# Down projection of a decoder layer: two more Strassen k pairs in its first pair of column groups, and its activation sums made by GpSimd

## The chip, the cores and the metric

The kernel runs on one core of one Trainium2 chip. The metric is the device time of one execution in microseconds. TensorE (PE in the profile) multiplies; its weight loads are a row of their own (PEld) and overlap its matmuls. VectorE (DVE), ScalarE (ACT) and GpSimd (POOL) work element by element, SyncE (SP) issues DMAs. Each engine runs its own instructions in the order of the program, and they wait for each other by semaphores.

## What is computed

One hybrid decoder layer over 256 tokens of width 2048: a mixer (attention heads beside a gated short convolution), cross-attention into 256 memory tokens, and a dense SwiGLU feed-forward layer, each with an RMS norm ahead of it and a residual add, and a last RMS norm. The change is in the last product:

```python
D_MODEL = 2048
D_FF = -(-(8 * D_MODEL) // (3 * 256)) * 256      # 5632
def swiglu(h, w_gate, w_up, w_down):
    return (jax.nn.silu(h @ w_gate) * (h @ w_up)) @ w_down
...
        x = x + swiglu(h, w_gate[l], w_up[l], w_down[l])
    return rms_norm(x, g_final)
```

## The kernel before

**Products.** A float32 product is made of three matmuls on rounded operands: high part times high part, high times low, low times high. A weight tile `raw` (128 partitions, two k blocks of 512 columns, 512 KB) comes by DMA from one stream; ACT rounds it to `whi` (line 1141), DVE subtracts `wlo = raw - whi` (line 1602), and PE multiplies. `raw`, `whi` and `wlo` are rings of four buffers (`RING`). ACT's cast of step v waits until PE has used step v-4; DVE's split waits for the cast; SP loads the next tile into a slot of `raw` when its last reader on DVE is done. ACT and DVE run `LEAD` = 2 steps ahead in their programs.

**The down projection.** Its k axis has 44 blocks of 128, in 22 pairs (numbered 0 to 21); the 2048 output columns are four groups of 512, taken as two pairs of groups, one after the other. `DOWN_ORDER` is an order written out by hand, one tuple for each pair of groups: "D8" is k pair 8 in the plain way, two steps (one for each group) of 12 matmuls; "A18" and "B18" are one such step each. "S0" is k pair 0 by Strassen's scheme: the 2 x 2 blocks (two k blocks and two token tiles on one side, two k blocks and two column groups on the other) are multiplied with seven products in place of eight, of three matmuls each: 21 matmuls in place of 24.

**An S step** has four parts, each a step of the rings, with 1, 2, 2 and 2 products. For part 0 ACT casts half a tile, and DVE makes a weight sum in `raw` (line 1597), the split (1602) and a second sum (1605). Part 1 has a split of a whole tile and then a third sum, `wsum` (1609). Part 2 casts and splits what now stands in the second tile, part 3 casts and splits `wsum`. SP loads into the slot of the first tile when `wsum` is made, and into that of the second when part 2 is split. Part 0 of the next S step needs both of these next tiles.

**Activation forms.** The S steps also need sums of the activations `fhi + flo`. They are made in four batches of two k pairs (`FORM_BATCH`): `down_sums(b)` makes a 128 x 1024 sum into `silu` (line 1634) and four 128 x 256 sums into `dsum` (1637, 1638, 1640, 1642), `down_forms(b)` on ACT casts them (1170, 1171), and `down_lows(b)` on DVE makes their low parts (1649, 1650). `FORMS_AT = {step: batch}` sets the place: after step i on DVE the sums, after step i+1 on ACT the casts, after step i+2 on DVE the low parts. PE waits for a batch (`d_lo`) at part 0 of the S steps. Batch b's sums wait for the low parts of batch b-1. POOL has no work in this stage until two small roots at the very end (line 479).

After the last S step of a pair of groups, `down_combine` adds the products up on DVE; the plain steps that follow in the order run beside it.

Of the kernel before, what the change touches and what calls it, by code (L numbers as in the profile page):

```python
# [21 lines left out]
TT = SEQ // P  # L22
# [11 lines left out]
KS = 2  # L34
# [17 lines left out]
G_DN = G_FF + 2 * NFC  # L52
# [19 lines left out]

DOWN_QUADS = 8
FORM_BATCH = 2
DOWN_ORDER = (("D6", "D7", "D8", "S0", "D9", "S1", "D10", "D11", "S2", "D12", "S3", "D13", "D14", "S4", "D15", "S5",
               "D16", "D17", "D18", "D19", "D20", "D21"),
              ("D8", "D9", "D10", "S0", "D11", "S1", "D12", "S2", "D13", "S3", "D14", "S4", "D15", "S5", "D16", "S6",
               "D17", "S7", "A18", "A19", "A20", "A21", "B18", "B19", "B20", "B21"))
DOWN = []
DOWN_TILES = []  # L80
for pair, order in enumerate(DOWN_ORDER):
    for name in order:
        q = int(name[1:])
        if name[0] == "S":
            n = len([1 for place in DOWN if place[4] == 0])
# [10 lines left out]
             for g in range(4)]  # L96
DOWN_BANKS = (2, 4, 0, 6)
PRODUCT_BANKS = ((0, 1, 7, 6), (2, 3, 4, 5))
FORMS_AT = {0: 0, 14: 1, 28: 2, 50: 3}
SQUARES_AT = {PAIR_AT[1] + 1: 0, PAIR_AT[1] + 2: 1, GROUP_END[2] + 2: 2}  # L100
ADDS_AT = {at - 1: g for at, g in SQUARES_AT.items()}
GAINS_AT = {PAIR_AT[1] + 2: 0, PAIR_AT[1] + 3: 1, GROUP_END[2] + 3: 2}
# [46 lines left out]
def build(nc, stream, x, xT, mem, memT, params, pos, inv_freq, g_final, out):  # L149
    f32, f32r, i32 = mybir.dt.float32, mybir.dt.float32r, mybir.dt.int32  # L150
    ALU, ACT, AX = mybir.AluOpType, mybir.ActivationFunctionType, mybir.AxisListType
    ds = bass.ds
    ctx = ExitStack()
    with ctx:
# [3 lines left out]
        def sb(name, shape, dt=f32, at=None):  # L158

            size = 4 * int(np.prod(shape[1:]))  # L160
            spot = place if at is None else at
            line = LINE if size >= LINE else 64
            where = -(-spot[0] // line) * line
            spot[0] = where + -(-size // 64) * 64
            return nc.alloc_sbuf_tensor_at(name, shape, dt, offset=where)
# [6 lines left out]
        def sem(name):  # L172
            return ctx.enter_context(nc.semaphore(name))
# [88 lines left out]
        fhi = sb("fhi", [P, FF // P, SEQ], f32r, at=fat)  # L262
        flo = sb("flo", [P, FF // P, SEQ], f32r, at=fat)
        silu = sb("silu", [P, TT, GC], at=fat)
# [9 lines left out]
        dsum = sb("dsum", [P, QUAD_PARTS, FORM_BATCH, P], at=sums_at)  # L274
        junk2 = sb("junk2", [P, GC], at=sums_at)
        assert sums_at[0] <= fat[0]
        dsrc = silu[:].rearrange("p t n -> p (t n)").rearrange("p (n k t m) -> p n k t m", n=FORM_BATCH, k=KS, t=TT)
# [50 lines left out]
        d_src, d_sums, d_made, d_hi, d_lo = (sem(n) for n in ("d_src", "d_sums", "d_made", "d_hi", "d_lo"))  # L328
# [17 lines left out]
        def await_out(eng, g, gi=0):  # L346

            eng.wait_ge(evacuated[g % 2], gi + (g // 2 + 1))
# [69 lines left out]
        def _(pool):  # L418
# [12 lines left out]
            def root(n):  # L431

                pool.wait_ge(var_ready, n + 1)
                nc.gpsimd.tensor_tensor(rstd[:, n, :], vpe[:, n, :], mhalf[:], ALU.pow).then_inc(rstd_ready, 1)
# [39 lines left out]
                                            ALU.subtract).then_inc(merged_conv, 1)  # L474
            root(2)
            root(3)
            for t in range(TT):
                pool.wait_ge(fvar_ready, t + 1)
                nc.gpsimd.tensor_tensor(frstd[:, t:t + 1], fvar[:, t:t + 1], mhalf[:, 0:1], ALU.pow).then_inc(frstd_ready, 1)
# [402 lines left out]
        def _(act):  # L882
# [12 lines left out]
            def unit(u, k, col, hi, ui=0, uk=0):  # L895

                act.wait_ge(unit_T, ui + (u + 1))
                bank = ps[:, unit_bank(u), :].rearrange("p (k t) -> p k t", k=KS)
                if col is None:
                    done = nc.scalar.activation(hi[:, ds(uk + k, KS), :], bank, ACT.Copy)  # L900
                else:
                    if U_H3 <= u < U_H3 + QUADS:
                        for n in range(KS):
                            nc.scalar.activation(araw[:, u - U_H3, n], bank[:, n, :].rearrange("p (t m) -> p t m", t=TT),
                                                 ACT.Copy, scale=gain(col + k + n))
                    for n in range(KS):
                        done = nc.scalar.activation(hi[:, k + n, :], bank[:, n, :], ACT.Copy, scale=gain(col + k + n))
                done.then_inc(unit_hi, 1)
# [318 lines left out]
            for i in range(len(DOWN)):  # L1227
                down_cast(i + LEAD)
                if i == LEAD:
                    act.wait_ge(step_used, V_DN)  # L1230
                    act.dma_start(gfin[:], g_final.partition_broadcast(P)).then_inc(gfin_loaded, 16)
                    for n in range(2 * (NFC - 1), 2 * NFC):
                        unit(U_FF + n, KS * n, None, fhi)
                if i - 1 in FORMS_AT:
                    down_forms(FORMS_AT[i - 1])
                for pair in range(2):
# [28 lines left out]
        def _(dve):  # L1265
            vec = nc.vector
# [278 lines left out]
            for j in range(J_XO + 1, J_FF):  # L1545
                split(j + LEAD)
                n = j - J_XO
# [74 lines left out]
                    r, pair, q, n, part = DOWN[i]  # L1622
                    part_split(V_DN + i, J_DN + r, part, DOWN_SUMS + 3 * n)

            def down_sums(b):

                k = slice(2 * KS * b, 2 * KS * (b + 1))
                flat = silu[:].rearrange("p t n -> p (t n)")
                a11, a21, a12, a22 = (dsrc[:, :, k_, t, :] for k_ in range(KS) for t in range(TT))
                if b:  # L1630
                    dve.wait_ge(d_lo, b)
                else:
                    await_out(dve, G_DN - 1)
                vec.tensor_tensor(flat, fhi[:, k, :].rearrange("p k t -> p (k t)").bitcast(f32),
                                  flo[:, k, :].rearrange("p k t -> p (k t)").bitcast(f32), ALU.add).then_inc(d_src, 1)
                dve.wait_ge(d_src, b + 1)
                vec.tensor_tensor(dsum[:, 0], a21, a22, ALU.add).then_inc(d_sums, 1)
                vec.tensor_tensor(dsum[:, 2], a21, a11, ALU.subtract)
                dve.wait_ge(d_sums, 2 * b + 1)
                vec.tensor_tensor(dsum[:, 1], dsum[:, 0], a11, ALU.subtract).then_inc(d_sums, 1)  # L1640
                dve.wait_ge(d_sums, 2 * b + 2)
                vec.tensor_tensor(dsum[:, 3], a12, dsum[:, 1], ALU.subtract).then_inc(d_made, 1)

            def down_lows(b):

                here = slice(FORM_BATCH * b, FORM_BATCH * (b + 1))
# [91 lines left out]

            for i in range(len(DOWN)):
                down_split(i + LEAD)  # L1740
                if i in FORMS_AT:
                    down_sums(FORMS_AT[i])
                if i == LEAD:
                    for n in range(2 * (NFC - 1), 2 * NFC):
                        unit(U_FF + n, KS * n, None, fhi, flo)
                if i - 2 in FORMS_AT:
                    down_lows(FORMS_AT[i - 2])
                for pair in range(2):
                    if i == LAST_QUAD[pair] + QUAD_PARTS:
                        down_combine(pair)  # L1750
                if i in ADDS_AT:
                    for t in range(TT):
                        add_result(ADDS_AT[i], t)
                if i in GAINS_AT:
                    dve.wait_ge(gfin_loaded, 16)
                    for t in range(TT):
                        dve.wait_ge(part_ready, TT * GAINS_AT[i] + t + 1)
                        gain_result(GAINS_AT[i], t)
# [66 lines left out]
```

## Time and profile before

| | us |
|---|---|
| median of 3 runs | 1200.52 (1200.32 to 1200.54) |
| the profiled execution, its own time | 1199.66 |
| its span, first to last instruction | 1198.0 |
| busy: PE, DVE, ACT, POOL | 1186.2, 930.4, 673.6, 83.5 |
| mean granted TensorE clock | 0.998 of full speed |

A matmul's row in the timeline shows when it began and how long it was in the pipeline (0.39 us); the next one begins 0.23 us later, so matmuls overlap and the distance between starts is what one costs. For the same reason a short pause of PE does not show as idle time, but as a longer distance between two starts. The same goes for DVE: a row of 1.22 us is followed by the next 1.14 us after its start.

### The profile page before, as it was taken

What the parts mean: (1) busy time and instruction counts of PE and PEld (TensorE: products, weight loads), DVE (VectorE), ACT (ScalarE), POOL (GpSimd) and SP (SyncE); (2) the same over time, 40 slices, a digit from 0 to 9 for tenths busy, and PEclk for the clock granted to TensorE, in tenths of its full rate; (3) what the DMA queues carried; (4) which work ended last, traced back from release to release, by engine and by line L of the source; (5) the groups of instructions that cost most, each with busy time, mean ns of one, the idle gap of its engine ahead of it and who ended that gap; (6) DMA issues with size and microseconds to landing.
All of it is one profiled execution on the core that took longest, in us unless ns stands there. A gap on an engine that the chain in (4) does not pass through costs nothing.

```text
span 1198.0 us, 16405 instructions
## 1 busy us (share of the span) xinstructions
PE 1186.2 (99%) x5421; PEld 983.2 (82%) x5421; DVE 930.4 (78%) x1171; ACT 673.6 (56%) x881; POOL 83.5 (7%) x89
## 2 busy tenths in 40 slices
PE   9999999999999999999999999999999999999997
PEld 8888888888888888788888888888888888888885
DVE  5755555557855666999899899989989989978886
ACT  5665555446644575666556555655555555545553
POOL 0042332200210000000000000000000000000000
PEclk9999999999999999999999999999999999999999
DMA  9865455556555544465666567556656666665663
GB/s 339 295 211 173 162 175 177 173 175 225 163 191 182 189 158 141 148 222 176 203 201 199 186 199 229 169 196 205 210 181 204 209 212 199 214 218 173 202 206 141
DMA packets 65851, 234.52 MB, mean 196 GB/s; under 512 B 7696, under 2 KB 8464, under 8 KB 65424
## 3 DMA queue, kind: packets, MB, share of 16 engines
q1 hardware_dynamic: 63072, 225.60, 57.4%
q10 hardware_dynamic: 2736, 8.35, 1.9%
q8 instruction: 26, 0.43, 0.2%
q14 instruction: 17, 0.14, 0.0%
HBM read 231.83 MB, written 2.10 MB: 195 GB/s over the span
## 4 chain that ended last, share of the span: by engine, by line
PE 92%; DVE 4%; DMA 1%; ACT 1%; issue 1%; SPq 0%; POOLq 0%; POOL 0%; ACTq 0%; DVEq 0%
PE ps L489 24%; PE ps L491 24%; PE ps L490 23%; PE ps L732 6%; PE ps L734 6%; PE ps L733 6%; DVE wlo L1602 2%; DMA raw<-w_stream 1%; PE ps L521 1%; DVE wsum L1609 0%; ACT whi L1141 0%; PE ps L604 0%; PE ps L559 0%; PE ps L564 0%; PE ps L688 0%
## 5 line engine op out<-in xcount | busy, mean ns | idle before, releaser
L1141 ACT ACTIVATE whi<-raw 128x1024 fp32r<-128x1024 f32 (+1 forms) x309 | 303.7, 992 | 214.6 <-PE ps L491 94.2
L1602 DVE TENSOR_TENSOR wlo<-raw,whi 128x1024 fp32r<-128x1024 f32 (+1 forms) x309 | 345.3, 1137 | 25.2 <-ACT whi L1141 24.4
L1271 DVE TENSOR_TENSOR wlo<-raw,whi 128x1024 fp32r<-128x1024 f32 x160 | 198.7, 1245 | 112.7 <-ACT whi L893 112.5
L489 PE MATMUL ps<-whi,ahi 128*128 128x512 f32 x600 | 235.6, 393 | 0.0
L491 PE MATMUL ps<-whi,alo 128*128 128x512 f32 x600 | 233.7, 390 | 0.0
L490 PE MATMUL ps<-wlo,ahi 128*128 128x512 f32 x600 | 233.5, 389 | 0.0
L893 ACT ACTIVATE whi<-raw 128x1024 fp32r<-128x1024 f32 x160 | 168.4, 1058 | 107.1 <-PE ps L491 94.7
L489 PE MATMUL ps<-whi,bhi 128*128 128x512 f32 x448 | 180.1, 402 | 0.8 <-DVE wlo L1271 0.7
L491 PE MATMUL ps<-whi,blo 128*128 128x512 f32 x448 | 175.1, 391 | 0.0
L490 PE MATMUL ps<-wlo,bhi 128*128 128x512 f32 x448 | 174.5, 389 | 0.0
L491 PEld LDWEIGHTS ps<-whi,alo 128*128 128x128 f32 x600 | 112.6, 188 | 23.7
L490 PEld LDWEIGHTS ps<-wlo,ahi 128*128 128x128 f32 x600 | 112.7, 188 | 22.8
L489 PEld LDWEIGHTS ps<-whi,ahi 128*128 128x128 f32 x600 | 112.7, 188 | 22.6
L491 PEld LDWEIGHTS ps<-whi,blo 128*128 128x128 f32 x448 | 84.1, 188 | 18.3
L489 PEld LDWEIGHTS ps<-whi,bhi 128*128 128x128 f32 x448 | 84.2, 188 | 17.6 <-issue 1.6
L490 PEld LDWEIGHTS ps<-wlo,bhi 128*128 128x128 f32 x448 | 84.3, 188 | 16.4
L489 PE MATMUL ps<-whi,fhi 128*128 128x512 f32 x240 | 93.7, 390 | 0.2 <-DVE wlo L1602 0.2
L491 PE MATMUL ps<-whi,flo 128*128 128x512 f32 x240 | 93.4, 389 | 0.0
L490 PE MATMUL ps<-wlo,fhi 128*128 128x512 f32 x240 | 93.4, 389 | 0.0
L1141 ACT ACTIVATE whi<-wsum 128x1024 fp32r<-128x1024 f32 x47 | 49.9, 1062 | 68.5 <-PE ps L491 49.0
L1602 DVE TENSOR_TENSOR wlo<-wsum,whi 128x1024 fp32r<-128x1024 f32 x47 | 57.6, 1225 | 36.3 <-ACT whi L1141 35.6
L1609 DVE TENSOR_TENSOR wsum<-raw 128x1024 f32<-128x1024 f32 x47 | 57.2, 1217 | 0.0
(244 smaller groups left out, 1489.9 us busy)
## 6 DMA issues: line engine op xcount, KB each, us to landing
raw<-w_stream SPq DMA_DIRECT2D x422, 512.0 KB, 4.1
res<-x_in ACTq DMA_DIRECT2D x4, 512.0 KB, 8.0
stage<-mem_in ACTq DMA_DIRECT2D x4, 512.0 KB, 6.4
proj<-mem_T ACTq DMA_DIRECT2D x2, 1024.0 KB, 9.4
stage<-x_T SPq DMA_DIRECT2D x7, 256.0 KB, 6.9
y_out<-res SPq DMA_DIRECT2D x4, 320.0 KB, 3.0
raw<-w_stream SPq DMA_DIRECT2D x4, 256.0 KB, 4.7
gfin<-g_final ACTq DMA_DIRECT2D x1, 1024.0 KB, 4.8
```

The source lines that it names most:

```text
L489: nc.tensor.matmul(bank, lhsT=a_h, rhs=w_h, start=start, stop=False)
L490: nc.tensor.matmul(bank, lhsT=a_h, rhs=w_l, start=False, stop=False)
L491: return nc.tensor.matmul(bank, lhsT=a_l, rhs=w_h, start=False, stop=stop)
L521: done = nc.tensor.transpose(bank[:, n, t * P:(t + 1) * P], src[:, t, (k + n) * P:(k + n + 1) * P], ident[:])
L732: nc.tensor.matmul(ps[:, bank, :], lhsT=a[0], rhs=w[0], start=start, stop=False)
L733: nc.tensor.matmul(ps[:, bank, :], lhsT=a[0], rhs=w[1], start=False, stop=False)
L734: return nc.tensor.matmul(ps[:, bank, :], lhsT=a[1], rhs=w[0], start=False, stop=stop)
L893: nc.scalar.activation(tile_pair(whi, j), tile_pair(raw, j), ACT.Copy).then_inc(hi_ready, 1)
L1141: nc.scalar.activation(whi_here, src, ACT.Copy).then_inc(hi_ready, 1)
L1271: vec.tensor_tensor(tile_pair(wlo, j), tile_pair(raw, j), tile_pair(whi, j).bitcast(f32), ALU.subtract).then_inc(lo_ready, 1)
L1602: vec.tensor_tensor(lo_here, src, hi_here.bitcast(f32), ALU.subtract).then_inc(lo_ready, 1)
L1609: vec.tensor_tensor(wsum[:].rearrange("p (h n) -> p h n", h=2), both, b22.unsqueeze(1).to_broadcast([P, 2, GC]), ALU.subtract).then_inc(w_ ...
```

## The change

The first tuple of `DOWN_ORDER` holds eight S steps in place of six: k pairs 6 and 7 move from D to S. Its start is D8 to D11 in place of D6 to D8, and from S0 on each S step is followed by one D step, up to S7. The batches of forms move with it, to steps 3, 11, 23 and 35. The sums of all four batches are made by GpSimd, with the same waits. The casts on ACT and the low parts on DVE stay where `FORMS_AT` puts them.

```diff
-DOWN_ORDER = (("D6", "D7", "D8", "S0", "D9", "S1", "D10", "D11", "S2", "D12", "S3", "D13", "D14", "S4", "D15", "S5",
-               "D16", "D17", "D18", "D19", "D20", "D21"),
+DOWN_ORDER = (("D8", "D9", "D10", "D11", "S0", "D12", "S1", "D13", "S2", "D14", "S3", "D15", "S4", "D16", "S5",
+               "D17", "S6", "D18", "S7", "D19", "D20", "D21"),
...
-FORMS_AT = {0: 0, 14: 1, 28: 2, 50: 3}
+FORMS_AT = {3: 0, 11: 1, 23: 2, 35: 3}
...
+            def down_sums(b):
+
+                k = slice(2 * KS * b, 2 * KS * (b + 1))
+                flat = silu[:].rearrange("p t n -> p (t n)")
+                a11, a21, a12, a22 = (dsrc[:, :, k_, t, :] for k_ in range(KS) for t in range(TT))
+                if b:
+                    pool.wait_ge(d_lo, b)
+                else:
+                    await_out(pool, G_DN - 1)
+                nc.gpsimd.tensor_tensor(flat, fhi[:, k, :].rearrange("p k t -> p (k t)").bitcast(f32),
+                                  flo[:, k, :].rearrange("p k t -> p (k t)").bitcast(f32), ALU.add).then_inc(d_src, 1)
+                pool.wait_ge(d_src, b + 1)
+                nc.gpsimd.tensor_tensor(dsum[:, 0], a21, a22, ALU.add).then_inc(d_sums, 1)
...
+            for b in range(len(FORMS_AT)):
+                down_sums(b)
...
-                if i in FORMS_AT:
-                    down_sums(FORMS_AT[i])
```

On POOL, the difference at the end of its program (names before the arrow are written, those behind it read); the five rows of a batch come four times, ahead of the last roots:

```order
 L434 TENSOR_TENSOR rstd<-vpe,mhalf 128x2 x2
-L479 TENSOR_TENSOR tail<-tail,mhalf 128x1 x2
+L486 TENSOR_TENSOR silu<-fhi,flo 128x1024
+L489 TENSOR_TENSOR dsum<-silu 128x256
+L490 TENSOR_TENSOR dsum<-silu 128x256
+L492 TENSOR_TENSOR dsum<-dsum,silu 128x256
+L494 TENSOR_TENSOR dsum<-silu,dsum 128x256
```

So POOL now has twenty instructions beside the first pair of groups.

On DVE, before, from the split of S1's last part (`wlo<-wsum,whi`) on: the sums of batch 1 after one split of D10, and its low parts two splits later, between D10 and D11:

```order
L1602 TENSOR_TENSOR wlo<-wsum,whi 128x1024
L1602 TENSOR_TENSOR wlo<-raw,whi 128x1024
L1634 TENSOR_TENSOR silu<-fhi,flo 128x1024
L1637 TENSOR_TENSOR dsum<-silu 128x256
L1638 TENSOR_TENSOR dsum<-silu 128x256
L1640 TENSOR_TENSOR dsum<-dsum,silu 128x256
L1642 TENSOR_TENSOR dsum<-silu,dsum 128x256
L1602 TENSOR_TENSOR wlo<-raw,whi 128x1024 x2
L1649 TENSOR_TENSOR flo<-dsum,fhi 128x2x128
L1650 TENSOR_TENSOR dfl<-dsum,dfh 128x3x256
```

On DVE, now, from the split of S1's part 1 on (line 1623 is the split, 1630 `wsum`, 1651 and 1652 the low parts):

```order
L1623 TENSOR_TENSOR wlo<-raw,whi 128x1024
L1630 TENSOR_TENSOR wsum<-raw 128x1024
L1651 TENSOR_TENSOR flo<-dsum,fhi 128x2x128
L1652 TENSOR_TENSOR dfl<-dsum,dfh 128x3x256
L1623 TENSOR_TENSOR wlo<-raw,whi 128x1024
L1623 TENSOR_TENSOR wlo<-wsum,whi 128x1024
L1623 TENSOR_TENSOR wlo<-raw,whi 128x1024 x2
```

The sums are gone, and the low parts of batch 1 now stand inside an S step, between its parts 1 and 2; those of batches 2 and 3 stand likewise inside S3 and S5, those of batch 0 ahead of S0.

On ACT, before, around the forms of batch 1, which stand in a row of plain casts of D10 and D11:

```order
L1141 ACTIVATE whi<-raw 128x1024 x2
L1170 ACTIVATE fhi<-dsum 128x2x128
L1171 ACTIVATE dfh<-dsum 128x3x256
L1141 ACTIVATE whi<-raw 128x1024 x2
L1141 ACTIVATE whi<-raw 128x512
```

On ACT, now:

```order
L1162 ACTIVATE whi<-raw 128x512
L1191 ACTIVATE fhi<-dsum 128x2x128
L1192 ACTIVATE dfh<-dsum 128x3x256
L1162 ACTIVATE whi<-raw 128x1024 x2
L1162 ACTIVATE whi<-wsum 128x1024
```

They now stand inside S1, between the casts of its parts 0 and 1 (inside S3 and S5 for batches 2 and 3).

## Rows read from the trace of the kernel before

**Rows 1.** Page, busy time by engine: us, share of the span, instructions.

```profile
PE 1186.2 (99%) x5421; PEld 983.2 (82%) x5421; DVE 930.4 (78%) x1171; ACT 673.6 (56%) x881; POOL 83.5 (7%) x89
```

**Rows 2.** Timeline of PE, down projection: start, duration, line, tiles, idle before.

```profile
993.04 0.39 PE L491 MATMUL ps<-whi,flo 128*128 128x512 f32 x1
993.42 0.50 PE L489 MATMUL ps<-whi,fhi 128*128 128x512 f32 x1
...
1019.16 0.39 PE L491 MATMUL ps<-whi,flo 128*128 128x512 f32 x1
1019.73 0.50 PE L489 MATMUL ps<-whi,fhi 128*128 128x512 f32 x1 [0.18 <-DVE wlo L1602]
1020.07 0.40 PE L490 MATMUL ps<-wlo,fhi 128*128 128x512 f32 x1
```

**Rows 3.** Timeline of DVE, first pair of groups: low parts, sums, splits.

```profile
968.52 0.41 DVE L1649 TENSOR_TENSOR flo<-dsum,fhi 128x256 fp32r<-128x256 f32 x1
...
969.72 1.22 DVE L1602 TENSOR_TENSOR wlo<-raw,whi 128x1024 fp32r<-128x1024 f32 x1
...
989.42 1.22 DVE L1634 TENSOR_TENSOR silu<-fhi,flo 128x1024 f32<-128x1024 f32 x1
...
992.14 1.22 DVE L1602 TENSOR_TENSOR wlo<-raw,whi 128x1024 fp32r<-128x1024 f32 x1
```

**Rows 4.** Timeline of ACT around the forms of batch 1.

```profile
992.26 0.42 ACT L1170 ACTIVATE fhi<-dsum 128x256 fp32r<-128x256 f32 x1 [3.11 <-DVE dsum L1642]
...
993.32 1.99 ACT L1141 ACTIVATE whi<-raw 128x1024 fp32r<-128x1024 f32 x2
```

**Rows 5.** Timeline of DVE, second pair of groups: S0, D11, S1, D12, S2.

```profile
1087.82 1.23 DVE L1602 TENSOR_TENSOR wlo<-raw,whi 128x1024 fp32r<-128x1024 f32 x1 [1.15 <-ACT whi L1141]
...
1090.60 1.22 DVE L1602 TENSOR_TENSOR wlo<-raw,whi 128x1024 fp32r<-128x1024 f32 x1 [0.42 <-ACT whi L1141]
...
1100.81 1.22 DVE L1602 TENSOR_TENSOR wlo<-raw,whi 128x1024 fp32r<-128x1024 f32 x1
...
1106.93 0.69 DVE L1597 TENSOR_TENSOR raw<-raw 128x512 f32<-128x512 f32 x1
...
1111.01 1.22 DVE L1602 TENSOR_TENSOR wlo<-raw,whi 128x1024 fp32r<-128x1024 f32 x1
```

**Rows 6.** Timeline of ACT, same stretch: casts for part 0 of S steps.

```profile
1095.89 0.63 ACT L1141 ACTIVATE whi<-raw 128x512 fp32r<-128x512 f32 x1 [0.56 <-DMA raw<-w_stream]
...
1106.20 0.63 ACT L1141 ACTIVATE whi<-raw 128x512 fp32r<-128x512 f32 x1 [0.68 <-DMA raw<-w_stream]
...
1147.80 1.58 ACT L1141 ACTIVATE whi<-raw 128x512 fp32r<-128x512 f32 x2 [1.47 <-DMA raw<-w_stream]
```

**Rows 7.** Timeline of PE's weight loads: the first of part 2 of S0, of S1.

```profile
1093.78 0.19 PEld L732 LDWEIGHTS ps<-whi,fhi 128*128 128x128 f32 x1
...
1103.98 0.19 PEld L732 LDWEIGHTS ps<-whi,fhi 128*128 128x128 f32 x1
```

**Rows 8.** Timeline of POOL in the attention stage, beside rows 9.

```profile
74.73 0.74 POOL L441 TENSOR_TENSOR rtmp<-proj,sin 128x256 f32<-128x256 f32 x1
75.42 1.73 POOL L441 TENSOR_TENSOR rtmp<-proj,cos 128x256 f32<-128x256 f32 x1
...
99.09 1.66 POOL L441 TENSOR_TENSOR rtmp<-proj,cos 128x256 f32<-128x256 f32 x1
```

**Rows 9.** Timeline of DVE in the same stretch.

```profile
74.88 1.67 DVE L1271 TENSOR_TENSOR wlo<-raw,whi 128x1024 fp32r<-128x1024 f32 x1 [2.01 <-ACT whi L893]
...
97.98 0.16 DVE L1411 TENSOR_TENSOR small<-small 128x2 f32<-128x2 f32 x1 [1.97 <-ACT osc L1011]
98.93 1.23 DVE L1271 TENSOR_TENSOR wlo<-raw,whi 128x1024 fp32r<-128x1024 f32 x1 [0.58 <-ACT whi L893]
100.07 0.70 DVE L1416 TENSOR_TENSOR small<-small 128x2 f32<-128x2 f32 x1
```

**Rows 10.** Page, DMA issues: KB each, median us from issue to landing.

```profile
raw<-w_stream SPq DMA_DIRECT2D x422, 512.0 KB, 4.1
```

More of the change, by code:

```diff
@@ L476, in _ @@
             root(3)
+            def down_sums(b):
[10 more added lines that the diff above has]
+                nc.gpsimd.tensor_tensor(dsum[:, 0], a21, a22, ALU.add).then_inc(d_sums, 1)
+                nc.gpsimd.tensor_tensor(dsum[:, 2], a21, a11, ALU.subtract)
+                pool.wait_ge(d_sums, 2 * b + 1)
+                nc.gpsimd.tensor_tensor(dsum[:, 1], dsum[:, 0], a11, ALU.subtract).then_inc(d_sums, 1)
+                pool.wait_ge(d_sums, 2 * b + 2)
+                nc.gpsimd.tensor_tensor(dsum[:, 3], a12, dsum[:, 1], ALU.subtract).then_inc(d_made, 1)
+            for b in range(len(FORMS_AT)):
+                down_sums(b)
             for t in range(TT):
@@ L1623, in down_split @@
                     part_split(V_DN + i, J_DN + r, part, DOWN_SUMS + 3 * n)
[L1625 to L1642, printed above, removed]
             def down_lows(b):
```

## The prediction, made before the changed kernel was run

> **What bounds the kernel.** I read the busy times first: PE is busy for 1186.2 of 1198.0 us [rows 1], so only what shortens PE's work, or makes it wait, counts. Then the timeline of PE: starts of matmuls are 0.227 us apart (from rows 7: part 2 of S1 begins 10.20 us after part 2 of S0, and 21 + 24 = 45 matmuls lie between; 10.20 / 45). Two places in the first pair of groups are wider: 0.38 us between starts and then 0.33, and 0.57 and then 0.34 [rows 2]. That is 0.25 and 0.45 us of waiting, in sum 0.7, each time for a split of DVE. So PE has almost no slack to win, and the question is how far ahead of it DVE runs in the S steps. That I read from the second pair of groups, where eight S steps alternate with D steps without any forms between them: the new order of the first pair, undisturbed.
>
> **The change, part by part.**
>
> 1. *Matmuls.* Two k pairs take 21 in place of 24: 2 x 3 x 0.227 = **-1.4 us** on PE. Its cover, DVE and ACT, is the subject of the rest.
>
> 2. *Sums leave DVE.* A batch holds DVE from 989.42 to 992.14, 2.7 us [rows 3]. The two waits of [rows 2] fall right behind batches 1 and 2; with the sums gone they go: **-0.7 us**. Before the first S step nothing else is late: eight plain steps give the splits time.
>
> 3. *The chain that paces S steps in a row.* PE does an S and a D step in 10.20 us. But part 0 of an S step waits for a tile whose DMA is issued when part 2 of the S step before is split. That split ends at 1100.81 + 1.22 = 1102.03 [rows 5], ACT's next part-0 cast begins, out of an idle time ended by the DMA, at 1106.20 [rows 6], 4.2 us later (a load takes 4.1 [rows 10]), DVE's next part 0 at 1106.93, and its part 2 ends at 1111.01 + 1.22 = 1112.23 [rows 5]. From 1106.20 to 1147.80 are four periods [rows 6], 10.4 us each. So the chain DMA, ACT, DVE, DMA takes 0.1 to 0.2 us more than PE, has no idle time to give, and what delays it is not made up before the S steps end. Before, the first pair had a second D step after every other S; now none. Seven periods at 0.15: 1.0 us.
>
> 4. *Low parts move into the chain.* They take 968.52 to 969.72, 1.2 us [rows 3]. Batches 1, 2, 3 now stand between parts 1 and 2 of S1, S3, S5, ahead of the split that releases the DMA: 3 x 1.2 = 3.6 us. Batch 0 lies ahead of S0, where there is room: 0.
>
> 5. *Casts of the forms move into the chain.* They take 992.26 to 993.32, 1.06 us [rows 4], between ACT's casts of parts 0 and 1. DVE's part 0 covers most: it keeps DVE until 2.5 us after ACT's part-0 cast began (1106.20 to about 1108.74, three half tiles), and cast, forms and cast need 0.5 + 1.06 + 1.15 = 2.7. 0.2 each, 0.6 us.
>
> 6. *GpSimd against DVE.* Rows 8 and 9 go together. POOL's instruction of 74.73 ran; DVE's split of 74.88 took 1.67 in place of 1.22 us, so it got going at 75.33, 0.60 after POOL's start. POOL's next took 1.73 in place of 0.74, so it waited until 76.41, 1.08 after the split got going. The second place is the same: POOL's of 99.09 waits 0.92, to 100.01, and DVE's small sum of 100.07, right behind its split, takes 0.70 in place of 0.16. So an instruction of one holds back the other until it is through (0.60 us for 128 x 256 on POOL, 1.08 for a split on DVE), and they take turns even when DVE has the next one ready. All of DVE's instructions in S steps are of the kind held back there. For POOL's 128 x 1024 sum no row exists: between 0.6 (if the hold doesn't grow) and 4 x 0.60 = 2.4; I take 2.3, since POOL's time must grow with the elements. A batch then holds DVE back for up to 2.3 + 4 x 0.6 = 4.7 us, against 2.7 that it took on DVE itself. What DVE can absorb is its idle time.
>
> The Trainium skill ("SBUF — State Buffer", "Who interferes with whom") speaks against this change: a DVE instruction with two SBUF inputs and a GpSimd instruction that reads SBUF exclude each other for a whole instruction. By it the long sum holds DVE for all of its time, as I take it; if the hold were 0.6 us it would be the second rival below. The rows agree on the exclusion, for short ones.
>
>    - Batch 0 starts when the last `up` is done, beside plain steps. Each DVE step has over 1 us of idle time there: 0.
>    - Batch 1 is released by the low parts of batch 0, just ahead of S0, so it runs through S0's parts 0 to 2. DVE's idle time in them is 1.15 + 0.42 = 1.6 us [rows 5]: 4.7 - 1.6 = 3.1 us later at part 2.
>    - Batches 2 and 3 are released inside S1 and S3, just ahead of part 2. DVE does that split, then the long sum holds it, then they take turns through part 3, two plain splits and the next part 0. DVE's own work to there is 3 x 1.14 = 3.4 us, POOL's 2.3 + 3 x 0.6 = 4.1: 7.5, where the chain has 4.9 (1102.03 to 1106.93). That is 2.6, and 0.3 net for the fifth sum inside part 0 (it can start as soon as the cast is there): 2.9 each, 5.8 us. POOL's own waits hurt nobody: each batch is done some 10 us before ACT casts it.
>
>    Sum of delays on the chain, from part 2 of S0 to part 2 of S7: 1.0 + 3.6 + 0.6 + 3.1 + 5.8 = 14.1 us. PE's slack there: S0's part 2 is split at 1090.60 + 1.22 = 1091.82 [rows 5], PE's first weight load of it is at 1093.78 [rows 7]: 1.95 us. What is more, PE waits: 14.1 - 1.95 = **+12.1 us**.
>
> After S7 six plain steps follow and `down_combine`, as before; 6 x 2.7 us of PE cover its 5 us.
>
> Sum: -1.4 - 0.7 + 12.1 = **+10.0 us**. On the profiled execution's own 1199.66 this is 1209.7; it lies 0.86 under the median of the runs, so 1210.5 for the median.
>
> **The rivals.**
>
> *No hold on DVE, chain still tight* (12%): terms 3 to 5 stay, 5.2 - 1.95 = 3.3 us of waiting, sum +1.2: 1201.7. Against it stand both pairs of rows in [rows 8, 9].
>
> *A short hold* (18%): every POOL instruction holds DVE for 0.6 us, the long one too. Batch 1: 3.0 - 1.6 = 1.4. Batches 2, 3: 3.4 + 2.4 - 4.9 + 0.3 = 1.2 each. 5.2 + 1.4 + 2.4 = 9.0, less 1.95 = 7.1; sum +5.0: 1205.5. For it: no row shows a longer hold.
>
> *The chain has room* (5%): a load into a freed tile lands soon enough for DVE to catch up in each period, and DVE isn't held. It decides where the chain's period falls under 10.2 us by what the forms add, 1.4 us for each two S steps, that is where loads land 0.7 us sooner than in [rows 6, 10]. Then only terms 1 and 2 are left: -2.1, 1198.4. That is 0.18%, and no route in this profile gains more, so even the kindest case is hardly faster.
>
> *A longer hold* (8%): POOL slower than in proportion, or its steps late as well, and delays that also move the DMAs of plain tiles: over 1213.5.
>
> The forecast itself, 1207.5 to 1213.5, has 57%: the hold of the long sum between 1.8 and 2.7 us moves three batches by 2 us, and the period's excess of 0.1 to 0.2 by 0.7.
>
> **The numbers.** 1210.5 us. The range, 1202.0 to 1214.0, takes in the short hold and most of the rest. About 0.2% (2.4 us) is what a measurement of this kernel can tell from no change. Faster by more: 3%. Within it: 14% (no hold, the chain has room). Slower: 83%.
>
> **What would show it.** PE's waits for the split should go from 2 to a dozen or so, most at `wlo` of parts 2 and 3 of S1 to S5, by some 12 us; none in the second pair of groups. POOL's long sum should take over 2 us, its short ones 0.7 or up to 1.9 where they wait, and DVE's splits beside them up to 3.5 in place of 1.22. If PE's waits lie at parts 2 only and DVE's rows keep their 1.22, the no-hold rival is right. If batches 2 and 3 leave no wait at part 3, the hold is short. I am wrong altogether if part-0 casts in the first pair are not preceded by a wait for the DMA or for DVE.

## The result: slower by 7.8 us, with the profile after

| | before | changed |
|---|---|---|
| median, us (4 runs each) | 1200.42 (1199.21 to 1200.54) | 1208.24 (1207.64 to 1209.28) |
| the profiled execution's own time, us | 1199.66 | 1208.20 |
| its span, us | 1198.0 | 1206.0 |
| mean granted TensorE clock | 0.998 | 0.998 |

The ratio is 1.0070, with a 95% interval of 1.0058 to 1.0082. The forecast was 1210.5 us in a range of 1202.0 to 1214.0.

The page of the changed kernel, busy time by engine as in [rows 1]:

```profile
PE 1186.4 (98%) x5415; PEld 980.5 (81%) x5415; DVE 944.1 (78%) x1161; ACT 676.4 (56%) x885; POOL 119.5 (10%) x109
```

DVE has ten instructions fewer than before and is busy for 13.7 us longer. PE has six matmuls fewer and the same busy time, since a short pause of it does not show as idle, in a span that is 8 us longer. What PE waited for is seen in the waits of its weight loads in the down projection (what was waited for, us in total, times, longest), here of the changed kernel:

```profile
PEld ps L753 <- DVE wlo L1623: 10.5, 8, 2.1
PEld ps L510 <- DVE wlo L1623: 0.9, 2, 0.4
```

Before, the same view of the same stretch has one line:

```profile
PEld ps L489 <- DVE wlo L1602: 1.0, 2, 0.6
```

From the distances between the ends of PE's steps, the waits of the changed kernel take 10.3 us: 0.64 at part 2 of S0; 1.07 and 1.97 at parts 2 and 3 of S1; 0.45 at part 2 of S2; 1.50 and 1.98 in S3; 0.50 in S4; 1.44 in S5; twice 0.3 at the D step behind S1 and S3; 0.1 in small ones. There is none in S6 and S7 and none in the second pair of groups. So -1.4 (matmuls), -0.7 (the two waits of [rows 2], gone) and +10.3 make +8.2; the spans differ by 8.0.

The first five waits of over 0.5 us, in the timeline of PE's weight loads (start, duration; in brackets the idle time before and what ended it), S0 to S3:

```profile
983.45 0.19 PEld L753 LDWEIGHTS ps<-whi,fhi 128*128 128x128 f32 x1 [0.76 <-DVE wlo L1623]
...
994.72 0.19 PEld L753 LDWEIGHTS ps<-whi,fhi 128*128 128x128 f32 x1 [1.20 <-DVE wlo L1623]
...
998.05 0.19 PEld L753 LDWEIGHTS ps<-whi,dfh 128*128 128x128 f32 x1 [2.10 <-DVE wlo L1623]
...
1007.70 0.19 PEld L753 LDWEIGHTS ps<-whi,fhi 128*128 128x128 f32 x1 [0.58 <-DVE wlo L1623]
...
1019.41 0.19 PEld L753 LDWEIGHTS ps<-whi,fhi 128*128 128x128 f32 x1 [1.63 <-DVE wlo L1623]
```

Why the split came late at 998.05 stands in two timelines of the same kernel. POOL, batch 2, released by the low parts of batch 1:

```profile
993.61 3.30 POOL L486 TENSOR_TENSOR silu<-fhi,flo 128x1024 f32<-128x1024 f32 x1 [11.29 <-DVE dfl L1652]
996.99 1.59 POOL L489 TENSOR_TENSOR dsum<-silu 128x256 f32<-128x256 f32 x1
998.55 1.71 POOL L490 TENSOR_TENSOR dsum<-silu 128x256 f32<-128x256 f32 x1
1000.22 1.72 POOL L492 TENSOR_TENSOR dsum<-dsum,silu 128x256 f32<-128x256 f32 x1
1002.02 1.07 POOL L494 TENSOR_TENSOR dsum<-silu,dsum 128x256 f32<-128x256 f32 x1
```

And DVE beside it, from the split of S1's part 2 on:

```profile
993.45 1.22 DVE L1623 TENSOR_TENSOR wlo<-raw,whi 128x1024 fp32r<-128x1024 f32 x1
994.59 3.41 DVE L1623 TENSOR_TENSOR wlo<-wsum,whi 128x1024 fp32r<-128x1024 f32 x1
997.92 3.43 DVE L1623 TENSOR_TENSOR wlo<-raw,whi 128x1024 fp32r<-128x1024 f32 x2
1001.27 1.22 DVE L1618 TENSOR_TENSOR raw<-raw 128x512 f32<-128x512 f32 x1
```

These two are read together, row by row. POOL's long sum is given out at 993.61, while DVE's split of 993.45 runs until 994.67; its 3.30 us are 1.06 of waiting and some 2.2 of work. DVE's next split of the same size takes 3.41 in place of 1.22: 2.19 us of it are POOL's long sum. Then they take turns: POOL's short sums take 1.6 to 1.7 (0.74 alone), and DVE's two plain splits take 3.43 together in place of 2.35, 0.54 each. The last row, a weight sum over half a tile, takes 1.22 in place of the 0.68 of such a row alone, again 0.54.

### The profile page after: what moved, and what is told of

It reads as the page before. It is cut to its first block, busy times and chain, and to the rows that moved or that the text cites. A ratio compares the mean times of both kernels' runs of the same rounds, so it can differ in the third digit from the quotient of the medians.

```text
span 1206.0 us, 16411 instructions
## 1 busy us (share of the span) xinstructions
PE 1186.4 (98%) x5415; PEld 980.5 (81%) x5415; DVE 944.1 (78%) x1161; ACT 676.4 (56%) x885; POOL 119.5 (10%) x109
## 4 chain that ended last, share of the span: by engine, by line
PE 87%; DVE 7%; DMA 2%; ACT 2%; POOL 1%; issue 1%; SPq 0%; POOLq 0%; ACTq 0%; DVEq 0%
PE ps L510 22%; PE ps L512 22%; PE ps L511 22%; PE ps L753 5%; PE ps L755 5%; PE ps L754 5%; DVE wlo L1623 4%; DMA raw<-w_stream 2%; PE ps L542 1%; DVE wsum L1630 1%; ACT whi L1162 1%; DVE raw L1618 0%; DVE raw L1626 0%; PE ps L625 0%; PE ps L580 0%
## 5 line engine op out<-in xcount | busy, mean ns | idle before, releaser
L1623 DVE TENSOR_TENSOR wlo<-raw,whi 128x1024 fp32r<-128x1024 f32 (+1 forms) x311 | 355.9, 1165 | 18.6 <-ACT whi L1162 17.3
L1623 DVE TENSOR_TENSOR wlo<-wsum,whi 128x1024 fp32r<-128x1024 f32 x49 | 64.4, 1314 | 34.7 <-ACT whi L1162 33.7
L510 PE MATMUL ps<-whi,fhi 128*128 128x512 f32 x224 | 87.5, 391 | 0.0
L511 PE MATMUL ps<-wlo,fhi 128*128 128x512 f32 x224 | 87.2, 389 | 0.0
L512 PE MATMUL ps<-whi,flo 128*128 128x512 f32 x224 | 87.2, 389 | 0.0
L1630 DVE TENSOR_TENSOR wsum<-raw 128x1024 f32<-128x1024 f32 x49 | 60.1, 1227 | 0.0
```

The costliest lines, as they stand in the source:

```text
L510: nc.tensor.matmul(bank, lhsT=a_h, rhs=w_h, start=start, stop=False)
L511: nc.tensor.matmul(bank, lhsT=a_h, rhs=w_l, start=False, stop=False)
L512: return nc.tensor.matmul(bank, lhsT=a_l, rhs=w_h, start=False, stop=stop)
L1623: vec.tensor_tensor(lo_here, src, hi_here.bitcast(f32), ALU.subtract).then_inc(lo_ready, 1)
L1630: vec.tensor_tensor(wsum[:].rearrange("p (h n) -> p h n", h=2), both, b22.unsqueeze(1).to_broadcast([P, 2, GC]), ALU.subtract).then_inc(w_ ...
```

## The experiments

The kernel before ran beside them each time: 1200.22 us (13 runs) beside order_only, pool_only, no_sums and quarters; 1199.87 (33 runs) beside pool_writes, no_sums_out, spread and spaced7; 1199.66 (7 runs) beside order_again, pool_late0 and spaced7_pool. Waits are those of PE's weight loads in the down projection.

### One half of the change at a time: order_only, pool_only

*order_only* has the new order and `FORMS_AT`, and DVE makes the sums as before:

```diff
-            for b in range(len(FORMS_AT)):
-                down_sums(b)
...
                 down_split(i + LEAD)
+                if i in FORMS_AT:
+                    down_sums(FORMS_AT[i])
```

> The change without GpSimd: the new order with eight S steps and the new places of the forms, but the four batches of sums back on DVE, at steps 3, 11, 23 and 35. Theory (the chain DMA, ACT, DVE that paces S steps in a row has no room, so whatever is put on DVE between S0 and S7 is paid): the low parts (1.2 us) and the forms' casts stay inside S1, S3, S5, and 2.7 us of sums stand ahead of S1, S3, S5 in an idle time of some 1.5 us. About 2.4 us of waiting at S1 and 2.8 at each of S3 and S5, 8 us in all, less 1.4 us of matmuls and the 0.7 us of waits that go: about 1206.3, and PE's waits at part 2 of S1, S3, S5 only. Rival 1, the order alone is the cause and GpSimd harmless: 1208, as the whole change. Rival 2, GpSimd alone is the cause: 1199 to 1200.

Measured: 1207.86 us (4 runs, 1206.17 to 1209.06), ratio 1.0067 (1.0050 to 1.0083). Its waits:

```profile
PEld ps L732 <- DVE wlo L1602: 8.0, 6, 2.2
```

They are pairs, about 0.28 and 2.1 us by step ends, in S1, S3 and S5, and nothing elsewhere.

*pool_only* is the kernel before, with its order, and GpSimd makes the sums:

```diff
+            for b in range(len(FORMS_AT)):
+                down_sums(b)
...
                 down_split(i + LEAD)
-                if i in FORMS_AT:
-                    down_sums(FORMS_AT[i])
```

> The change without its order: six S steps and the places of before, but the sums on GpSimd. Theory (each GpSimd instruction holds DVE back for its whole length): batch 0 is ready some 5 us later than on DVE, and ACT, which waits for it one step after the sums, holds its casts of D7 and D8 back: some 2 us of waiting there. Batch 1 then runs through S0, some 2.5 us more. Batches 2 and 3 run beside D steps in a row, which take most of it: 0 to 1.5 us each. The two waits of 0.7 us go. 1203 to 1208, most likely 1206. Rival 1, the order alone is the cause: 1199.7 to 1200.4. Rival 2, GpSimd alone: 1208 or more.

Measured: 1209.08 us (4 runs, 1208.51 to 1212.08), ratio 1.0079 (1.0063 to 1.0096), above the 1203 to 1208 that was expected. Some 1.7 us of its 9.75 us of waits lie in the two steps of D8, where 2 were expected (in the new order the prediction had seen room for batch 0). What goes beyond the expected range lies in S0, beside batch 1: three waits of 4.7 us in sum, where I had expected 2.5. ACT's row for batch 0:

```profile
967.93 0.42 ACT L1191 ACTIVATE fhi<-dsum 128x256 fp32r<-128x256 f32 x1 [7.80 <-POOL dsum L494]
```

ACT stood still for 7.8 us behind one cast of a form, and with it every cast of weights queued after it.

**What follows.** Each half alone costs about as much as both. There are two separate prices: in the new order the sums disturb the chain of S steps whether DVE or GpSimd makes them, and with GpSimd as the maker the order of before is disturbed too. They don't add up, since a sum is made once.

### The sums taken out, and GpSimd kept busy without reading: no_sums, pool_writes

```diff
+                if b:
+                    pool.memset(spark_pair[:, 1:2], 0.0).then_inc(d_made, 1)
+                    return
                 nc.gpsimd.tensor_tensor(flat, fhi[:, k, :].rearrange("p k t -> p (k t)").bitcast(f32),
```

> The whole change, but the sums of batches 1, 2 and 3 are left out: GpSimd makes batch 0 and then only signals, so that the casts and low parts of the later batches take what batch 0 left in the buffer. DVE, ACT, PE and the DMAs do all that they do in the changed kernel. Theory: only the chain's own excess, low parts and casts inside S1, S3, S5 are left: 1.6 us of waiting by the loads as they came in the changed kernel's trace (3.4 to 4.7 us from a split to the next cast), 3.3 us by my prediction's terms; 1200.0 to 1201.7. All of GpSimd's part in the change is then 6.5 to 8 us. Rival 1 (the order alone): 1207 to 1208. Rival 2 (GpSimd alone, and the chain has room): 1198.4.

Measured: 1199.97 us (10 runs), ratio 0.9997 (0.9988 to 1.0007). The waits left are those of the chain alone:

```profile
PEld ps L756 <- DVE wlo L1626: 2.7, 3, 1.7
```

By step ends 2.4 us: 0.37 in S3, 0.45 in S4, 1.54 in S5. -1.4 -0.7 +2.4 is +0.3; the spans differ by 0.3, the medians by -0.25.

*pool_writes* puts a chain of memsets of `silu` in the place of each batch left out:

```diff
+                    sizes = [1024] * 3 + [640] * 4
+                    for n, size in enumerate(sizes):
+                        pool.memset(flat[:, 0:size], 0.5).then_inc(d_src, 1)
+                        pool.wait_ge(d_src, 1 + len(sizes) * (b - 1) + n + 1)
```

> As the run without the sums of batches 1 to 3 (1199.97), but in their place GpSimd is kept busy for about as long as the sums took it undisturbed (some 5.5 us a batch) with fills of the same buffer, which write SBUF and read nothing; the later batches again take what batch 0 left. If GpSimd holds DVE back whenever it works on SBUF: 1207 to 1208, and DVE's splits beside the fills take up to twice their 1.22 us. If only its reads do so (the Trainium skill, SBUF - State Buffer, section Who interferes with whom, says so; no row so far shows it): 1200.0, and the splits keep 1.22 us. I expect the second, with 75%. GpSimd's signal comes later than without sums, but ACT asks for it some 10 us later still, so lateness alone gives nothing.

Measured: 1200.22 us (10 runs), ratio 1.0001 (0.9992 to 1.0011). POOL's row of one such batch:

```profile
974.52 5.75 POOL L489 MEMSET silu<- 128x1024 f32 x7 [4.71 <-DVE dfl L1659]
```

and DVE's rows inside it:

```profile
977.41 1.23 DVE L1630 TENSOR_TENSOR wlo<-raw,whi 128x1024 fp32r<-128x1024 f32 x1 [1.15 <-ACT whi L1169]
978.55 1.22 DVE L1637 TENSOR_TENSOR wsum<-raw 128x1024 f32<-128x1024 f32 x1
```

**What follows.** GpSimd was busy for 5.75 us a batch and DVE's rows kept their 1.22. The kernel's time beside it is that without sums. So it is neither POOL's being busy nor its semaphores, but its reading, that holds DVE here. The Trainium skill ("SBUF — State Buffer", "Who interferes with whom") says this of writes: a DVE instruction with two SBUF inputs contends with a GpSimd instruction that reads SBUF, not with one that only writes it. The trace agrees, with 1.22 us beside the memsets and 3.41 beside the sum.

### The long sum in four pieces: quarters

```diff
-                nc.gpsimd.tensor_tensor(flat, fhi[:, k, :].rearrange("p k t -> p (k t)").bitcast(f32),
...
+                for n in range(4):
+                    part_n = slice(256 * n, 256 * (n + 1))
+                    nc.gpsimd.tensor_tensor(flat[:, part_n], hf[:, part_n], lf[:, part_n], ALU.add).then_inc(d_src, 1)
+                pool.wait_ge(d_src, 4 * (b + 1))
```

> The whole change, but GpSimd's sum of 128 x 1024 is made as four of 128 x 256, so a batch is eight short instructions, none of which should hold DVE for over 0.6 us. Theory (what ends the wait at S2 and S4 is the sum of all that DVE was held, not the longest hold): waits move from part 3 of S1 and S3 to parts of S2 and S4, the total stays within 1 us, 1207.5 to 1209. Rival (the long hold just ahead of part 3, which has only 0.6 us of slack, is the cost, 2.0 us in each of S1 and S3): 4 us faster, 1204.2.

Measured: 1208.95 us (4 runs, 1207.83 to 1209.14), ratio 1.0069 (1.0052 to 1.0086). Its waits:

```profile
PEld ps L755 <- DVE wlo L1625: 11.7, 11, 1.7
PEld ps L512 <- DVE wlo L1625: 1.3, 3, 0.4
```

and DVE in S1, where the changed kernel has 3.41 and 3.43:

```profile
995.31 1.76 DVE L1625 TENSOR_TENSOR wlo<-wsum,whi 128x1024 fp32r<-128x1024 f32 x1
996.99 3.42 DVE L1625 TENSOR_TENSOR wlo<-raw,whi 128x1024 fp32r<-128x1024 f32 x2
1000.34 1.22 DVE L1620 TENSOR_TENSOR raw<-raw 128x512 f32<-128x512 f32 x1
1001.48 1.23 DVE L1625 TENSOR_TENSOR wlo<-raw,whi 128x512 fp32r<-128x512 f32 x1
```

**What follows.** One hold of 2.19 us became four of 0.54, spread over more of DVE's instructions: more waits, the longest of them shorter, the same time. What counts is the hold in sum. The time of 1204.2 us that stood against it is out by 4.7. It also says that the hold grows with the elements of POOL's instruction: 0.54 for 256, 2.19 for 1024. The short-hold rival had 3.0 us for a whole batch of five, where these make 2.19 + 4 x 0.54 = 4.35.

### The low parts out of the S steps: no_sums_out

```diff
-FORMS_AT = {3: 0, 11: 1, 23: 2, 35: 3}
+FORMS_AT = {3: 0, 14: 1, 26: 2, 38: 3}
```

> Again without the sums of batches 1 to 3, and besides, the forms' casts and low parts of batches 1 to 3 are moved by three steps, out of S1, S3 and S5 to the D step behind each (steps 14, 26, 38 in the table). Theory: put inside an S step, ahead of the split that releases the DMA, they cost; behind it they fall into DVE's wait for the load. The run without sums waits 2.4 us at S3, S4 and S5; here 0 to 0.5 us are left, 1197.8 to 1198.5. Rival (the eight S steps in a row are themselves too much for DVE, wherever the forms stand): no change, 1200.0.

Measured: 1200.37 us (10 runs, 1199.35 to 1202.22), ratio 1.0006 (0.9997 to 1.0016), beside no_sums' 1199.97: a miss. Its waits:

```profile
PEld ps L756 <- DVE wlo L1626: 2.1, 5, 0.8
PEld ps L513 <- DVE wlo L1626: 1.0, 2, 0.6
```

By step ends 2.3 us again, in other places (0.33, 0.61, 0.49 and 0.68 are the larger ones).

**What follows.** The place of the low parts isn't what costs. The second pair of groups has eight S steps one D step apart as well, without forms between them, and PE waits nowhere in it. So it is the work on the forms that such a stretch has no time for, inside the S steps or behind them. Between S1 and S2 the rows of no_sums_out show how it costs behind them, two of DVE with ACT's between:

```profile
995.28 1.22 DVE L1626 TENSOR_TENSOR wlo<-raw,whi 128x1024 fp32r<-128x1024 f32 x1 [0.77 <-ACT whi L1165]
...
996.47 1.58 ACT L1165 ACTIVATE whi<-raw 128x512 fp32r<-128x512 f32 x2 [0.28 <-DMA raw<-w_stream]
...
998.76 0.68 DVE L1621 TENSOR_TENSOR raw<-raw 128x512 f32<-128x512 f32 x1
```

ACT casts the forms ahead of D13's tiles, so DVE stands for 0.77 us; it then has D13's splits and the low parts to make, and begins part 0 of S2 2.3 us after ACT had the tile for it. I had expected all this to fall into the wait for the load.

Inside the S steps something else makes the low parts cheaper than their 1.2 us. These are DVE's splits of part 2 of S4 and S5 in no_sums, each with the row of ACT that waits for the load behind it:

```profile
1023.32 1.22 DVE L1626 TENSOR_TENSOR wlo<-raw,whi 128x1024 fp32r<-128x1024 f32 x1
...
1028.95 0.63 ACT L1165 ACTIVATE whi<-raw 128x512 fp32r<-128x512 f32 x1 [2.55 <-DMA raw<-w_stream]
...
1035.09 1.22 DVE L1626 TENSOR_TENSOR wlo<-raw,whi 128x1024 fp32r<-128x1024 f32 x1
...
1039.68 1.58 ACT L1165 ACTIVATE whi<-raw 128x512 fp32r<-128x512 f32 x2 [2.73 <-DMA raw<-w_stream]
```

Behind S4, without low parts, ACT goes on 4.4 us after the split's end (1024.54 to 1028.95); behind S5, where the low parts stand ahead of that split and the S step's other load was issued that much earlier, 3.4 us (1036.31 to 1039.68). In all six kernels that have the low parts inside S1 and S5 it is 3.2 to 3.4 behind both; in no_sums_out it is 4.0 to 5.4 behind S0 to S6. So 1.2 us of low parts ahead of the split cost some 0.3 net. That two loads issued further apart are back sooner after the second is my reading of it; no run moves the issue alone.

Behind S3 it is not so: 4.7 us in the changed kernel (1019.37 to 1024.03) and in no_sums (1013.90 to 1018.57). The DMA records in the traces have a candidate. In all seven kernels with the new order one 16 KB packet of the instruction queue falls into this load, and the load takes 4.7 to 5.7 us; behind S1 and S5 none does. In the changed kernel that packet runs from 1021.90 to 1022.78 and the load's last 4 KB from 1022.76 to 1023.20, with all its others through by 1022.41. That it is the cause isn't shown: behind S0 such a packet falls in as well, nearer to the load's end, and the load takes 3.9 to 4.6.

### The clock behind a long wait: order_again

In order_only's profile the granted clock fell once, at 1018.2 us, behind a wait of 2.1; behind the same wait in S1 and in S5 it stayed up. Its waits are 7.2 us by step ends, 3 less than in the whole change, and yet its time is the same. *order_again* is the same kernel once more.

> The run with the new order and the sums on DVE once more, to see PE's clock: there one wait of 3.2 us at part 2 of S3 was followed by 3.4 us at half the granted clock, and its four times lay between 1206.2 and 1209.1. If waits of over 2 us lower the clock now and then, times again spread over 2 to 3 us in this kernel, with mean clocks of 0.995 to 0.997, where the whole change (waits of at most 2.0 us in one piece) has 0.998 to 0.999 throughout. If it was a chance of that chip: 1205 to 1206, clock 0.998.

Measured: 1209.50 us (4 runs, 1207.82 to 1209.61), ratio 1.0079 (1.0062 to 1.0096), clock 0.995 in all four. (The wait in order_only that the expectation puts at 3.2 us is the 2.1 above.) This time the clock fell behind all three waits. The first, in three windows (stretch, PE's busy time, granted clock, DMA share, GB/s):

```profile
992.00:997.00 5.00, 3.18 (x14) 0.99 0.42 134
997.00:1000.20 3.20, 3.20 (x9) 0.50 0.77 266
1000.20:1005.00 4.80, 4.80 (x22) 0.98 0.45 136
```

and in PE's timeline, from the wait on:

```profile
995.48 0.50 PE L732 MATMUL ps<-whi,fhi 128*128 128x512 f32 x1 [1.82 <-DVE wlo L1602]
...
996.74 0.45 PE L734 MATMUL ps<-whi,dfl 128*128 128x512 f32 x1
996.98 0.63 PE L732 MATMUL ps<-whi,dfh 128*128 128x512 f32 x1
997.41 0.63 PE L733 MATMUL ps<-wlo,dfh 128*128 128x512 f32 x1
997.84 0.63 PE L734 MATMUL ps<-whi,dfl 128*128 128x512 f32 x1
```

**What follows.** Starts 0.43 us apart in place of 0.23: for 3.4 us PE runs at 1.2 GHz of its 2.4, and eight matmuls cost 8 x 0.2 = 1.6 us more. Three of these are 4.8. With them the sum closes: -1.4 -0.7 +7.2 +4.8 is +9.9 over the 1198.0 us span of before, and order_again's span is 1207.8. So a part of what the new order costs with sums on DVE is the clock: 4.8 us here, 1.6 in order_only's profile. The profiled changed kernel has no such stretch in the down projection; its waits are up to 2.0 us by step ends.

### Batch 0 two steps later: pool_late0

```diff
-FORMS_AT = {0: 0, 14: 1, 28: 2, 50: 3}
+FORMS_AT = {2: 0, 14: 1, 28: 2, 50: 3}
```

> As the run with the order of before and the sums on GpSimd (1209.08), but batch 0's casts and low parts two steps later, so that ACT does not stand waiting for GpSimd's first batch with the casts of D7 and D8 behind it (7.8 us idle there in that run). Theory (two things cost there: ACT's wait, and the hold on DVE): the 1.7 us of waits at D8 go, and what is left is the hold of batch 1 in S0 (2.5 to 4 us) and of batches 2 and 3 in S2 to S5 (3.3 us): 1205.5 to 1207. Rival (ACT's wait is the whole cost of batches 0 and 1): 1202.5. Rival (only the hold counts, ACT's wait is free): 1209.

Measured: 1205.67 us (4 runs, 1204.78 to 1206.04), ratio 1.0052 (1.0035 to 1.0069). The waits at D8 are gone, and the others stay, somewhat shorter in sum:

```profile
PEld ps L753 <- DVE wlo L1623: 6.8, 6, 2.9
PEld ps L510 <- DVE wlo L1623: 0.4, 1, 0.4
```

**What follows.** 2.9 of pool_only's 8.9 us went with batch 0's place (1.7 of them the two waits at D8); the other 6.0 are what sums on GpSimd beside a busy DVE cost in the order of before. A part of it may be the clock: the other three executions have a mean of 0.996 and take 0.6 to 1.3 us longer than the profiled one, and there is no trace of them. The longest wait here is longer than any above, 2.9 us, and in this profile the clock stayed up behind it. The length of a wait alone does not tell whether the clock falls; order_only and order_again, the same kernel with the same three pairs of waits, say so too.

### Towards a better version: spread, spaced7, spaced7_pool

*spread* is the kernel before with each batch's sums on DVE in two pieces, a step apart, and casts and low parts one step later:

```diff
                 if i in FORMS_AT:
-                    down_sums(FORMS_AT[i])
+                    down_sums(FORMS_AT[i], False)
+                if i - 1 in FORMS_AT:
+                    down_sums(FORMS_AT[i - 1], True)
...
-                if i - 2 in FORMS_AT:
-                    down_lows(FORMS_AT[i - 2])
+                if i - 3 in FORMS_AT:
+                    down_lows(FORMS_AT[i - 3])
```

> The kernel before, with its order and its sums on DVE, but each batch in two pieces: the 128 x 1024 sum after step i, the four small ones after step i+1, ACT's casts after i+2, the low parts after i+3. Theory: the two waits of 0.3 and 0.5 us behind batches 1 and 2 come from 2.7 us in one piece against 1.2 us of slack; in pieces of 1.1 and 1.6 us they vanish: 0.7 us less, 1199.5. Rival (DVE's total load decides, not where it stands): no change, 1200.2.

*spaced7* is spread with seven k pairs by Strassen's scheme, and two D steps behind every other S step:

```diff
-DOWN_ORDER = (("D6", "D7", "D8", "S0", "D9", "S1", "D10", "D11", "S2", "D12", "S3", "D13", "D14", "S4", "D15", "S5",
-               "D16", "D17", "D18", "D19", "D20", "D21"),
+DOWN_ORDER = (("D7", "D8", "D9", "S0", "D10", "S1", "D11", "D12", "S2", "D13", "S3", "D14", "D15", "S4", "D16", "S5",
+               "D17", "D18", "S6", "D19", "D20", "D21"),
...
-FORMS_AT = {0: 0, 14: 1, 28: 2, 50: 3}
+FORMS_AT = {0: 0, 14: 1, 28: 2, 42: 3}
```

> What theory would build: seven S steps (k pair 6 from D to S) with a second D step after each other S up to S5, so that each of batches 1, 2, 3 stands between two D steps in a row, sums on DVE in two pieces as in the run beside it, low parts outside S steps. 3 matmuls less, 0.7 us, and no waits: 1198.8. If the third batch between S5 and S6 makes new waits, 1199.5; if the order alone costs (rival 1), 1202 or more.

Measured: spread 1199.28 us (11 runs, 1198.19 to 1201.23), ratio 0.9995 (0.9986 to 1.0005); spaced7 1198.85 us (11 runs, 1198.34 to 1200.36), ratio 0.9996 (0.9987 to 1.0005). The waits of the kernel before, 1.0 us, become

```profile
PEld ps L732 <- DVE wlo L1602: 0.7, 2, 0.5
```

in spread, and in spaced7

```profile
PEld ps L732 <- DVE wlo L1602: 0.9, 3, 0.4
```

Both medians are near what was expected and under the one before, by 0.6 and 1.0 us, but neither interval leaves 1 out: no gain is shown. Either is some 9 us faster than the change.

*spaced7_pool* then asks whether GpSimd can be used at all: spaced7 with the sums on GpSimd, let go only when an S step's last split is done, and the casts of the forms another step later.

```diff
-FORMS_AT = {0: 0, 14: 1, 28: 2, 42: 3}
+FORMS_AT = {1: 0, 14: 1, 28: 2, 42: 3}
...
+                if b:
+                    pool.wait_ge(d_lo, b)
+                    pool.wait_ge(lo_ready, V_DN + {1: 14, 2: 28, 3: 42}[b] + 2)
```

> The seven S steps with second D steps between (1198.85 with its sums on DVE), but the sums on GpSimd, and each of batches 1, 2, 3 let go only when the split of part 3 of S1, S3, S5 is done, so that it runs beside four plain splits with DVE's idle time between them; casts and low parts at the step before the next S. Theory (the hold costs only where DVE has no idle time): 4.5 us of hold against some 4 us of idle time, 0 to 1 us of waiting for each batch: 1199.0 to 1201.5. If GpSimd's sums cost their hold wherever they run: 3 x 4.5 less little, 1206 or more. If GpSimd helps DVE at last: under 1198.8.

Measured: 1205.05 us (4 runs, 1204.39 to 1206.05), ratio 1.0047 (1.0030 to 1.0064): a miss, 3.5 us above the upper end. POOL, batch 1, from its first row to its last:

```profile
987.91 3.26 POOL L487 TENSOR_TENSOR silu<-fhi,flo 128x1024 f32<-128x1024 f32 x1 [19.20 <-DVE wlo L1624]
...
996.28 0.73 POOL L495 TENSOR_TENSOR dsum<-silu,dsum 128x256 f32<-128x256 f32 x1
```

DVE and ACT beside it:

```profile
987.68 7.92 DVE L1624 TENSOR_TENSOR wlo<-raw,whi 128x1024 fp32r<-128x1024 f32 x4
```

```profile
997.04 0.42 ACT L1192 ACTIVATE fhi<-dsum 128x256 fp32r<-128x256 f32 x1 [5.69 <-POOL dsum L495]
```

**What follows.** A batch that would take some 2.2 + 4 x 0.74 = 5.2 us alone takes 9.1 beside four splits, and the four splits 7.92 in place of 4.6. ACT reaches the cast of the form before it is made and stands for 5.7 us. I had reckoned the hold on DVE and forgotten that POOL is held back as much, and that ACT waits for POOL.

## Why the prediction was right, and where its sizes were off

**Direction and mechanism** held. The rows asked for at the prediction's end are there: PE's waits go from 2 to 10, most at `wlo` of parts 2 and 3 of S1 to S5, none in the second pair of groups; POOL's short sums take 0.74 to 1.72; DVE's splits beside it take up to 3.41.

**Terms 1 and 2**, -1.4 and -0.7: as forecast. The sums of waits and spans above, of the changed kernel, of no_sums and of order_again, close with both to within 0.2 us.

**Term 6, the hold, for each instruction.** The long sum holds DVE for 2.19 us, taken as 2.3 from bounds of 0.6 and 2.4; the short ones for 0.54, taken as 0.60 from [rows 8, 9]. That an instruction of one holds the other for its whole length stands, for the long sum too.

**Term 6, by batches.** Batch 0: nothing, as forecast. Batch 1: from DVE's first row of S0's part 0 to the end of its split of part 2, the changed kernel needs 9.67 us (973.73 to 983.40) and pool_writes, undisturbed, 7.04 (974.38 to 981.42): 2.6 us, forecast 3.1. Batches 2 and 3: from the end of the part 2 split of S1 to that of S2, 12.98 us beside 9.35 in no_sums, and from S3 to S4 12.96 beside 10.65. That is 3.6 + 2.3 = 5.9, forecast 5.8. The sum fits better than its parts do: I had 2.9 for each. The second is smaller because no_sums has the slow load behind S3 to wait for (10.65), and in the changed kernel the hold runs beside that load. So the good fit is in part luck.

**Terms 3 to 5, the chain**, were mis-sized as a sum. Terms 3 and 5 hold as terms: in the second pair of the changed kernel the period is 10.32 us on average from S0 to S6, beside PE's 10.20, and the forms' casts delay DVE's split of part 1 by some 0.2 us in each of S1, S3 and S5. Forecast 1.0 + 3.6 + 0.6 = 5.2 us of delay; no_sums, which has only these, shows 2.4 of waits, and with the 1.95 of slack that is 4.4. Two steps failed in it. The low parts were counted at their full 1.2, with the load behind them as long as ever; behind S1 and S5 it comes back 1.0 sooner (3.4 in place of 4.3 to 4.5). And seven periods were counted, where behind S5 the lag is made up: in S6 and S7 of the changed kernel the splits of part 2 are ready 1.2 and 1.0 us ahead of PE's matmuls. So a delay can be made up before the S steps end, against what term 3 says. And of the 4.4 some 1.3 are the slow load behind S3, which the prediction had no term for. no_sums_out adds that the place of the low parts, on which term 4 rested, makes no difference to PE: with them behind the S steps the waits are as long.

**The sum.** 4.4 + 2.6 + 5.9 = 12.9 of delay, forecast 14.1. Less the slack of 1.95 it is 11.0 of waits; the trace has 10.3. So of the 12.1 forecast, 0.8 went with terms 3 to 5 and 0.5 with batch 1, and 0.7 more I can't put down to a place. The chain's delays and those of the holds may overlap in S3 to S5; no run shows it.

**The rivals.** No hold (1201.7) falls with the 3.41. The short hold (1205.5) falls with it too, and with quarters. The chain has room (1198.4) falls with no_sums: its time is where that of the kernel before is, not 2 us below. Even with free sums the new order gains nothing, since the chain's 2.4 us eat the 2.1 of the two terms that gain.

**What the prediction didn't see.** It argued as if the sums on DVE had been the cheaper half of a trade. Under the new order they aren't: order_only costs 7.6 us (9.8 in order_again). In the new order the sums of a batch among the S steps make PE wait, as 2.7 us of DVE's work or as a hold of 4.4. Nor did it think of the granted clock as something that a wait can take down, which costs 1.6 us in order_only's profile and 4.8 in order_again's.

**Open:** whether the 16 KB packet is why the load behind S3 takes 4.7 us; what decides whether the clock falls behind a wait.

## What to carry to other kernels

Work moved from DVE to GpSimd isn't taken off DVE if both read two tensors from SBUF: each instruction of one held the other for its whole length here (2.19 us for GpSimd's long sum), so look for the moved work's time in the neighbour's rows, and give GpSimd writes. Whether a stretch in which DVE idles would do is not shown: beside spaced7_pool's four plain splits DVE was busy throughout. If an order spaces its heavy steps to let a load chain catch up, price that spacing (a period of the chain beside a period of PE) before trading it for fewer matmuls. And check what the next engine in line, here ACT with a program of its own, will meet first when a helper gets slower.

## What the runs showed of the hardware beyond what was expected

- **Reads collide, fills don't.** Seven memsets in a row on GpSimd, 5.75 us, left DVE's rows at 1.22; one sum of two SBUF tensors made one of them 3.41.
- **Strict turns.** Beside a DVE that always had its next instruction ready, GpSimd's batch of five took 9.1 us in place of some 5.2, and DVE's four splits 7.9 in place of 4.6.
- **The clock after a wait.** Behind pairs of waits of 0.4 and 2.25 us of the weight loads, the granted clock was 0.50 for 3.4 us, starting 0.2 to 1.5 us after PE was at work again, at a price of 1.6 us: three times out of three in order_again, once out of three in order_only, the same kernel. Behind 2.10 us in the changed kernel, and behind 2.94 us in pool_late0, it stayed at 1.0.
- **A load's time goes with when the one ahead of it was issued.** The same 512 KB were there 3.2 to 3.4 us after the slot came free where the load ahead had been issued 1.2 us earlier than usual (S1 and S5, six kernels), and 4.3 to 4.4 behind S2 and S4 of the changed kernel; behind S3, with a 16 KB packet of the instruction queue in it, it took 4.7 to 5.7 in seven kernels.
